# Where TensorE's transposes and stick-breaking products stand in a slot of the mixer stage

## What is computed

```python
h = rms_norm(x, norm_mix[l])
proj = h @ w_in[l]
u_ssm, q_nsa, kv_nsa, g_nsa, qkv_sb, g_merge = split_columns(proj)
o_ssm = s5_mixer(u_ssm, ...)                  # diagonal complex state space, 32 groups of 16 channels
o_nsa = nsa_mixer(q_b, k_b, v_b, gates_b, ...)  # compressed, selected and window attention, 8 heads
o_sb = stick_breaking_attention(q, k, v)      # 8 heads, strictly causal
branches = jnp.stack([o_ssm, o_nsa, o_sb], axis=2)
y = jnp.einsum('bsnc,ncd->bsnd', branches, w_branch[l])
x = x + jnp.sum(sigmoid(g_merge) * y, axis=2) @ w_out[l]
x = x + conv_ffn(rms_norm(x, norm_ffn[l]), ...)
```

## Time and profile before

| | us |
|---|---|
| three runs: median (lowest to highest) | 1009.65 (1008.5 to 1011.58) |
| the profiled execution: its own time | 1008.73 |
| the profiled execution: span from the first to the last instruction | 1007.0 |
| TensorE busy in the span | 946.4 (94%) |
| TensorE weight loads busy | 813.8 (81%) |
| VectorE busy | 741.7 (74%) |
| ScalarE busy | 565.7 (56%) |
| GpSimd busy | 344.1 (34%) |

### The profile page before, as it was taken

One profiled execution on the slowest core, in us unless ns is written; L12 is line 12 of the kernel. 1 busy time (PEld: TensorE's weight loads), 2 busy tenths in 40 slices (PEclk: granted clock), 3 DMA queues, 4 the chain that ended last, 5 costly groups with the idle time before them and its releaser, 6 DMA issues.

```text
span 1007.0 us, 16978 instructions
## 1 busy us (share of the span) xinstructions
PE 946.4 (94%) x6319; PEld 813.8 (81%) x6319; DVE 741.7 (74%) x1238; ACT 565.7 (56%) x905; POOL 344.1 (34%) x269
## 2 busy tenths in 40 slices
PE   5899899998998999999979998999999999999996
PEld 4799676676877999999879986777677699999995
DVE  5979999985666767677754679998747666666665
ACT  5335666757454655555554457666764555555554
POOL 0111666672320473155500137667516001111010
PEclk9899999999998999999989999999999999999999
DMA  8962433344454755555549432333544436555551
GB/s 227 256 185 85 128 124 127 109 101 167 141 171 138 206 180 196 169 205 168 160 122 266 126 126 92 118 127 110 152 151 162 137 129 207 188 187 177 198 167 42
DMA packets 135863, 156.82 MB, mean 156 GB/s; under 512 B 16400, under 2 KB 103032, under 8 KB 135800
## 3 DMA queue, kind: packets, MB, share of 16 engines
q1 hardware_dynamic: 135800, 155.98, 49.6%
HBM read 154.92 MB, written 1.05 MB: 155 GB/s over the span
## 4 chain that ended last, share of the span: by engine, by line
PE 71%; DVE 15%; ACT 7%; issue 3%; POOL 3%; DMA 1%; SPq 0%; POOLq 0%; DVEq 0%; ACTq 0%
PE pj L734 52%; PE bX L734 6%; PE bA L734 5%; DVE wl L1536 4%; PE bB L734 3%; PE bY L1074 1%; ACT wh L1245 1%; DVE s5x L1864 1%; PE bX L1063 1%; PE bY L734 1%; DVE gate L1552 1%; DVE bnat L1864 1%; POOL s5h L2112 1%; DVE work L1828 1%; PE bO L734 1%
## 5 line engine op out<-in xcount | busy, mean ns | idle before, releaser
L1536 DVE TENSOR_TENSOR wl<-ring,wh 128x1024 fp32r<-128x1024 f32 (+1 forms) x276 | 364.5, 1324 | 147.6 <-ACT wh L1245 146.2
L1245 ACT ACTIVATE wh<-ring 128x1024 fp32r<-128x1024 f32 (+1 forms) x276 | 288.9, 1048 | 256.7 <-PE pj L734 221.3
L734 PE MATMUL pj<-hh,wh 128*128 128x256 f32 x1024 | 295.9, 289 | 11.2 <-DVE wl L1536 8.3
L734 PE MATMUL pj<-hh,wl 128*128 128x256 f32 x1024 | 292.3, 285 | 0.0
L734 PE MATMUL pj<-hl,wh 128*128 128x256 f32 x1024 | 292.3, 285 | 0.0
L734 PEld LDWEIGHTS pj<-hh,wh 128*128 128x128 f32 x1024 | 199.4, 195 | 15.7 <-issue 14.0
L734 PEld LDWEIGHTS pj<-hl,wh 128*128 128x128 f32 x1024 | 199.4, 195 | 1.2 <-issue 0.5
L734 PEld LDWEIGHTS pj<-hh,wl 128*128 128x128 f32 x1024 | 199.1, 194 | 0.0
L734 PE MATMUL pj<-wh,hl 128*128 128x512 f32 (+1 forms) x416 | 171.1, 411 | 7.7 <-DVE hl L1558 3.7
L734 PE MATMUL pj<-wh,hh 128*128 128x512 f32 (+1 forms) x416 | 161.6, 388 | 0.0
L734 PE MATMUL pj<-wl,hh 128*128 128x512 f32 (+1 forms) x416 | 161.5, 388 | 0.0
(11 more groups left out here) (312 smaller groups left out, 1440.8 us busy)
## 6 DMA issues: line engine op xcount, KB each, us to landing
ring<-in_ffn_w_up SPq DMA_DIRECT2D x44, 1024.0 KB, 5.1
ring<-in_w_in SPq DMA_DIRECT2D x40, 1024.0 KB, 5.1
ring<-in_ffn_w_down SPq DMA_DIRECT2D x22, 1024.0 KB, 4.9
ring<-in_w_in SPq DMA_DIRECT2D x16, 512.0 KB, 5.2
ring<-in_w_branch SPq DMA_DIRECT2D x8, 1024.0 KB, 5.0
ring<-in_w_out SPq DMA_DIRECT2D x8, 1024.0 KB, 5.0
ring<-in_w_branch SPq DMA_DIRECT2D x8, 512.0 KB, 5.9
ring<-in_w_in SPq DMA_DIRECT2D x8, 256.0 KB, 4.5
```

Of the source, the lines that this page charges most:

```text
L734: return nc.tensor.matmul(o, a, b, start=start, stop=stop, skip_group_check=True)
L1245: A(dst, src, ACT.Copy).then_inc(w_hi.sem, 1)
L1536: TT(dst, src, hi.bitcast(F32), ALU.subtract).then_inc(w_lo.sem, 1)
```

## The change

Two steps, `nsa_turn` and `sb_rest`, which both run on the full array, are moved up to stand right behind the filler. `sb_scores` is moved ahead of `nsa_values`. The order in a slot is now F, T, R, X, S, Z, V, O, Y. No instruction is added or removed, no table is changed, and nothing but TensorE's own order differs.

```diff
                 for q in range(SLOTS):
                     filler(q)
+                    if q in NSA_T:
+                        nsa_turn(NSA_T[q])
+                    if q in SB_R:
+                        sb_rest(SB_R[q])
                     if q == CMP_HID:
...
                     if q in NSA_S:
                         nsa_scores(NSA_S[q])
-                    if q in NSA_T:
-                        nsa_turn(NSA_T[q])
+                    if q in SB_Z:
+                        sb_scores(SB_Z[q])
                     if q in NSA_V:
                         nsa_values(NSA_V[q])
-                    if q in SB_Z:
-                        sb_scores(SB_Z[q])
-                    if q in SB_R:
-                        sb_rest(SB_R[q])
                     if q in SB_O:
                         sb_values(SB_O[q])
```

## The result

| us | before | changed |
|---|---|---|
| median of 20 runs each | 1008.54 | 1011.14 |
| lowest to highest | 1007.55 to 1011.58 | 1008.97 to 1014.38 |
| profiled execution, its own time | 1008.73 | 1011.14 |
| its span | 1007.0 | 1009.4 |
| mean granted clock in it | 0.984 | 0.983 |

The changed kernel takes 1.0024 times as long, with an interval of 1.0016 to 1.0033. That is 2.6 us more, where +0.34 was said. (A correction to the part on the kernel: SLOTS is 2 x 28 = 56, not 60. No number rests on it.)

What follows compares the result with a forecast made beforehand. Bound: a chain through TensorE up to S4, DVE, then TensorE from slot 20's filler, and ACT from Z0. +0.20 and +0.14 us gave +0.34, 1009.07 for the profiled execution; against the median 1009.65 it said 1010.0, range 1007.6 to 1012.2.

Steps and rivals of the forecast that it cites:

- Prices of the steps: Start-to-start times on TensorE within a slot: filler to T 0.23, X to S 1.06, S to T 0.64 us.
- T to X: Step from T behind a filler to X, shown by no row before: taken as 0.53 us, bounds 0.35 and 0.59.
- Rival 2: T to X or S behind a filler costs only 0.35 us, like T to filler: 1008.55 us, chance 0.1.
- S4 within slot 15: The scores of pair 4, which DVE waits for, start 1.82 instead of 1.38 us behind the last filler start: +0.44.
- rival 1: DVE makes the delay of S4 good, so only TensorE's slots count: -0.15 us a layer, 1009.35 us, chance 0.2.
- Slots 20 and 25: T no longer stands between two steps on parts of the array: -0.15 us in each slot.
- slots 8, 10, 11 and 18: Each costs TensorE +0.03 us; only 10 and 11 in layer 0 lie on the path, +0.06 together.
- Together +0.34: Sum on the path of the mixer stages: +0.20 us in layer 0 and +0.14 in layer 1.
- The number itself: Forecast time of the whole changed kernel: 1010.0 us, against a median of 1009.65 before.
- Rival 3: TensorE's clock falls behind V0 of layer 1 (1011.2 us, chance 0.08), or also before both Y2 (1013.4, more often 0.07).

Runs made afterwards that it cites:

- e1_no15: The kernel before with T moved behind the filler in slots 8, 10, 11, 18, 20 and 25, not 15: 1008.82 us, ratio 0.9997.
- e1_change: The changed kernel run again, no edit, against the kernel before: 1011.87 us, ratio 1.0033.
- e1_before: The kernel before, unchanged, run again as a control: 1008.98 us, ratio 1.0003.
- e1_only15: The kernel before with T moved ahead of X and S in slot 15 alone: 1013.39 us, ratio 1.0048.
- e2_best: The kernel before with S ahead of X (slots 15, 22) and T behind the filler in slots 20 and 25 alone: 1009.5 us, ratio 1.0001.
- e3_late15: The order of before with fifteen spare transposes behind the filler of slot 44: 1012.14 us, ratio 1.0039.
- e2_sfirst: The kernel before with S ahead of X (slots 15 and 22), T where it was: 1008.96 us, ratio 0.9999.
- e4_warm2: The order of e2_best with spare matmuls cut to the length of TensorE's waits, against the kernel before: 1000.86 us, ratio 0.993.

## Why the prediction was right, and where not

The time lies in the range and the verdict within 0.3% is right; the step from the sum to the time is not.

- *Prices of the steps.* Right to the hundredth: 0.23, 0.53, 1.06, 0.64 as said. T to X, the edge that no row showed, is 0.53. Rival 2, the cheap edge, is out.
- *S4 within slot 15, +0.44 on the path.* Right: +0.43 and +0.49 when it stands alone. DVE did not make it good, and rival 1 is out.
- *Slots 20 and 25, -0.15 each.* Right in size: together with the small terms, e1_no15 gave -0.15 in layer 0 and -0.21 in layer 1. I did not measure slots 8, 10, 11 and 18 singly.
- *Together +0.34.* The order's part is +0.20 by V0 to Y2 in the first pair of traces, +0.45 by e1_change against e1_before. **The failed step is that this sum was then taken for the change in time** ("with +0.34 it is 1009.07"). It measured +2.6 us, and the 2.2 to 2.4 us beyond the order came in where the change moves no instruction and the clock is lower.
- *The number itself.* 1010.0 was said and 1011.14 measured, but part of that nearness is luck: the forecast stood on a median of three runs, 1009.65, and 20 runs gave 1008.54, 1.1 us less. The difference was missed by 2.3 us, the time by 1.1. The bounds of the range don't follow from the terms named for them either: rival 2 less the spread of the runs is 1007.4, one fall of the clock with the spread 1013.1.
- *Rival 3.* Its mechanism was the right one, and its price of 1.15 us a fall is of the size of what one cost at the end, somewhat more (993.95 to 994.77 before the last matmuls of the MLP, 1007.0 to 1009.4 at the end: 2.4 - 0.8 = 1.6). Its place was wrong: I looked behind the waits in the stage that the change touches, V0 of layer 1 and Y2, and had the argument "these waits don't grow". They need not grow. The fall came behind the last wait of the program, of an unchanged 2.3 us, and at the start of the MLP of layer 1, where 1.4 us went from Y2 to that wait. So its chance of 0.15 for all was too small, against a time that moved by 2.6.

Shown is that a delay of about half a microsecond a layer costs 3.0 to 4.7 us, with three makes of delay; that a wait of unchanged length is followed by a fall in some executions and not in others; and, for e1_before and e1_only15, that what came in beyond the order came in over the same matmuls at the lower level. Argued is that this holds for the medians too, since a trace is one execution of each kernel. At equal mean clock 1.4 us remain between the changed kernel and the one before, of which the order is 0.2 to 0.45, and a mean can't say where in the program the clock was low. Open is why a fall comes more often in the executions of the shifted kernels, and why executions of one and the same kernel differ in where it falls (before, the stretch at 808 is half as long as that at 806 in e1_before, the same program). The clock was not held up in the changed kernel itself; that was tried on the orders of before and of e2_best only.

## What to carry to other kernels

Where the engine that sets the end has waits of a few microseconds and its clock falls behind some of them, the sum of a reordering is not yet a time: list those waits up to the end of the program, also where nothing moves, since a shift in either direction can bring a fall behind one. Look at the granted clock behind the waits before tuning the order; independent matmuls cut to the length of the waits, with the order of e2_best, gave 0.7% here, where all reorderings alone gave nothing. Within a slot, put first what the other full engine waits for (S, for DVE), and only then what shares a part of the array.

## What the runs showed of the hardware

- The same wait of 2.34 us was followed by the lower clock or not: the windows from 985 to 1003 us show 1.00 (e1_before, it ended at 994.98), 0.91 (e1_only15, 997.03) and 1.00 (e3_late15, 998.75). The time of its end does not decide alone: the clock fell behind 993.92 (e2_sfirst) and not behind 993.95 (before).
- A stretch at the lower level costs what work falls into it: the same 128 x 256 matmuls start 0.21 us apart at the lower level and 0.12 at the upper (812.66 to 812.87 and 814.08 to 814.20 in e1_before), and the stretches at 806 in e1_before and at 809 in e1_only15, alike in length, differed by 1.24 us in what they cost, since the second lies 2.8 us later against the work.
- Delaying the work by 0.45 to 0.65 us a layer cost 3.0 to 4.7 us; delaying it by 1.6 us a layer 3.8.
- A spare product of 128 x 512 takes 0.87 us and shows as two matmuls of 0.44, where one product of the filler's rounded parts is one of 0.23; on the unit matrix, 128 columns, it is 0.11.
- The clock stayed up behind matmuls on the unit matrix, too: 44 of them filled the wait at the start of layer 0, of which the windows from 20 to 34 us show, before and then in e4_warm2:

```profile
20.00:34.00 14.00, 8.57 (x52) 8.14 (x52) 11.16 (x50) 7.49 (x13) 0.00 (x0) 0.76 0.79 167
```

```profile
20.00:34.00 14.00, 12.91 (x106) 12.27 (x105) 11.51 (x51) 8.56 (x14) 0.00 (x0) 1.00 0.78 169
```

The Trainium skill ("TensorE: Matmul & The Clock Gate", PE-mode transpose) says that the full clock doesn't engage for its transpose mode. Whether these instructions use that mode the trace doesn't say (it lists them as MATMUL of 128 x 128, line 860); here the clock was at 1.00 over them, so for matmuls issued like this the measurement decides.
